# The down projection of a gated feed-forward network as seven half-size block products

## The reference, cut to what matters

```
f = silu(gc) * u
y = f @ w_down
x = layer_norm(ALPHA * x1 + gate2 * y) * ln2_g + ln2_b
```

## Time and profile before

| what | us |
|---|---|
| median of 3 runs | 2961.08 (2960.83 to 2962.52) |
| the profiled execution | 2957.33 |
| its span, first to last instruction | 2955.5 |
| TensorE busy in the span | 2721.9 |
| VectorE busy | 1767.3 |
| ScalarE busy | 1231.5 |
| GpSimd busy | 471.4 |

### The profile page before, as it was taken

The page is one execution under the profiler, slowest core; times in us unless marked ns, Lnnn a source line. Parts: engine busy times, 40 slices in busy tenths (PEclk is TensorE's granted clock), DMA queues, the critical chain, the costliest instruction groups (busy, mean ns, idle before and its releaser), DMA issues. The chain is left out here.

```text
span 2955.5 us, 50052 instructions
## 1 busy us (share of the span) xinstructions
PE 2721.9 (92%) x17011; PEld 2471.3 (84%) x17011; DVE 1767.3 (60%) x3030; ACT 1231.5 (42%) x2612; POOL 471.4 (16%) x678
## 2 busy tenths in 40 slices
PE   5999999766999987996999999999999979999996
PEld 4999999655887866885999999999999968888875
DVE  4534332155999984777887876667666534352445
ACT  2211111125988971233555565556555522112121
...
GB/s 289 83 93 120 79 92 64 165 359 178 128 151 124 163 47 147 189 190 98 213 174 172 171 206 153 151 154 151 152 151 151 109 173 141 107 128 138 84 122 135
DMA packets 400710, 435.71 MB, mean 147 GB/s; under 512 B 122593, under 2 KB 293655, under 8 KB 397849
## 3 DMA queue, kind: packets, MB, share of 16 engines
...
q0 software_dynamic: 2304, 7.88, 0.8%
...
## 5 line engine op out<-in xcount | busy, mean ns | idle before, releaser
L2204 PE MATMUL fu_alpha<-fu_h,fu_w 128*128 128x384 f32 x3168 | 574.0, 335 | 17.6 <-DVE fu_h L2430 10.6
L2690 PE MATMUL fd_acc<-fd_w,fd_f 128*128 128x512 f32 x2376 | 544.0, 390 | 29.7 <-DVE fd_w L2718 18.8
L2204 PEld LDWEIGHTS fu_alpha<-fu_h,fu_w 128*128 128x128 f32 x3168 | 552.8, 188 | 20.3 <-issue 20.2
L2690 PEld LDWEIGHTS fd_acc<-fd_w,fd_f 128*128 128x128 f32 x2376 | 446.0, 188 | 127.6 <-issue 18.3
L2204 PE MATMUL fu_beta<-fu_h,fu_w 128*128 128x384 f32 x1584 | 287.3, 336 | 0.6 <-DVE fu_h L2430 0.6
L2204 PEld LDWEIGHTS fu_beta<-fu_h,fu_w 128*128 128x128 f32 x1584 | 277.1, 189 | 1.1 <-issue 1.1
L598 PE MATMUL pj_gps<-pj_ht,w_in 128*128 128x256 f32 x2160 | 268.8, 285 | 0.0
L598 PEld LDWEIGHTS pj_gps<-pj_ht,w_in 128*128 128x128 f32 x2160 | 263.5, 191 | 1.3
L2714 DVE TENSOR_TENSOR fd_f<-fd_f_stage,fd_f 128x512 fp32r<-128x512 f32 (+1 forms) x110 | 88.9, 810 | 283.6 <-ACT fd_f L2670 283.6
L2670 ACT CAST fd_f<-fd_f_stage 128x512 fp32r<-128x512 f32 (+1 forms) x110 | 63.4, 579 | 442.8 <-PE fd_acc L2690 391.8
L2404 DVE TENSOR_TENSOR fu_w<-up_w_stage,fu_w 128x512 fp32r<-128x512 f32 x264 | 181.4, 688 | 86.0 <-ACT fu_w L2268 84.0
(11 more groups left out here) (221 smaller groups left out, 4123.3 us busy)
## 6 DMA issues: line engine op xcount, KB each, us to landing
...
at_k<-k_t SPq DMA_DIRECT2D x28, 704.0 KB, 12.9
...
```

Source lines behind the costliest of these rows:

```text
L2204: mm = pe.matmul(out, w[x][:, j, k, :], b[y][:, j, k, :], start=opens and (k, x, y) == (0, HI, HI), stop=(k, x, y) == (KH - 1, LO, HI), sk ...
L2690: mm = pe.matmul(acc[:, t, at], f[a][:, slot, t * P:(t + 1) * P], w[b][:, w_at(st, slot), at], start=is_step(st, 0) and (a, b) == (HI, HI) ...
```

## The change: what it does

The product is cut into blocks: `f` of each pair of token tiles into 2 x 2 (two tiles of 128 tokens, two halves of the 2816 rows), `w_down` into 2 x 2 (two halves of rows, two halves of 512 columns). In place of eight block products, Strassen's scheme makes seven, out of sums and differences of blocks (`A_OF` for `f`, `B_OF` for the weights), and each output block is a signed sum of some of the seven (`COPIES`, `SUMS`). The loops are turned about: one product at a time (order 2, 3, 1, 4, 5, 7, 6) runs through all nine pairs of tiles, so a unit is one product for one pair, 63 in all, with 11 k-steps of three passes. The outputs of all 18 tiles are summed up in SBUF (`fd_res`). For each unit SP loads one block of `f`, and a second one into the single buffer `fd_f_more` where VectorE has to sum two. Weight slices go round in a ring of 17; GpSimd sums two weight slices where needed. An output block is complete after products 4, 5, 7 and 6 (`complete`: gate, residual, statistics); after 7 and 6 a whole tile is, and is normalised by ScalarE (with a scale and a shift from GpSimd), multiplied and shifted by GpSimd (`affine`) and stored. The first unit and the first product's weights are loaded in three pieces of k-steps (`PIECES`), the weights from ScalarE's queue; the very last tile is normalised by VectorE (`last_tile`, two operations of 1024 columns). `slices` and `slices_first` say in which unit the next product's weight slices are made.

```diff
@@ -2539,245 +2539,406 @@
 def ffn_down_phase(nc, f_t, w_down, x1, ln2_g, ln2_b, mod, out_all):
...
-    KEPT = 14
...
+    PAIRS = T_ALL // (2 * P)
+    KH = FT // 2
+    NH = D // 2
+    ORDER = (2, 3, 1, 4, 5, 7, 6)
+    A_OF = {1: ((0, 0), (1, 1), ALU.add), 2: ((1, 0), (1, 1), ALU.add), 3: ((0, 0), None, None), 4: ((1, 1), None, None),
+            5: ((0, 0), (0, 1), ALU.add), 6: ((1, 0), (0, 0), ALU.subtract), 7: ((0, 1), (1, 1), ALU.subtract)}
+    B_OF = {1: ((0, 0), (1, 1), ALU.add), 2: ((0, 0), None, None), 3: ((0, 1), (1, 1), ALU.subtract),
+            4: ((1, 0), (0, 0), ALU.subtract), 5: ((1, 1), None, None), 6: ((0, 0), (0, 1), ALU.add), 7: ((1, 0), (1, 1), ALU.add)}
+    COPIES = {2: ((1, 0, 1.0), (1, 1, -1.0)), 3: ((0, 1, 1.0),), 1: ((0, 0, 1.0),)}
+    SUMS = {3: ((1, 1, ALU.add),), 1: ((1, 1, ALU.add),), 4: ((0, 0, ALU.add), (1, 0, ALU.add)),
+            5: ((0, 0, ALU.subtract), (0, 1, ALU.add)), 7: ((0, 0, ALU.add),), 6: ((1, 1, ALU.add),)}
+    COMPLETE = {4: (1, 0), 5: (0, 1), 7: (0, 0), 6: (1, 1)}
+    UNITS = len(ORDER) * PAIRS
+    PIECES = ((0, 2), (2, 6), (6, KH))
+    AHEAD = 6
+    RING = KH + AHEAD
+    WSLOTS, XSLOTS, HSLOTS, BANKS = 3, 3, 2, 8
+    STAGED_AT = 12
+    FIRST_COMPLETE = ORDER.index(4) * PAIRS
+    FIRST_TAIL = ORDER.index(7) * PAIRS
...
+        with nc.sbuf_tensor("fd_f_raw", [P, XSLOTS, KH, P], F32) as f_raw:
+            pass
+        f_lo = sb("fd_f_lo", [P, XSLOTS, KH, P], F32R)
+        f_hi = sb("fd_f_hi", [P, HSLOTS, KH, P], F32R)
+        f_more = sb("fd_f_more", [P, KH, P])
+        w = [sb(f"fd_w{h}", [P, RING, NH], F32R) for h in (HI, LO)]
+        wst = sb("fd_w_stage", [P, WSLOTS, 2, NH])
+        res = sb("fd_res", [P, 2 * PAIRS, D])
+        xr = sb("fd_x1", [P, 2, NH])
...
+        acc = ps("fd_acc", [P, BANKS, NH])
...
+        def slices_first(u):
+            j, i = divmod(u, PAIRS)
+            return [j * KH + k for k in (KH - 2, KH - 1)] if i == 0 and 0 < j < len(ORDER) else []
+        def slices(u):
+            j, i = divmod(u, PAIRS)
+            if j >= len(ORDER) - 1:
+                return []
+            if i == PAIRS - 1:
+                return [(j + 1) * KH + k for k in range(AHEAD, KH - 2)]
+            return [(j + 1) * KH + i - 2] if 2 <= i < 2 + AHEAD else []
...
+                def load_unit(u):
+                    if u >= XSLOTS:
+                        sp.wait_ge(unit_done, u - XSLOTS + 1)
+                    load_f(u)
+                    if sums_f(u) and u:
+                        sp.wait_ge(f_summed, sum_count(u) - 1)
+                        load_more(u, more_staged)
+                def load_w(b):
+                    s = (b - KH) % WSLOTS
+                    if b - KH >= WSLOTS:
+                        sp.wait_ge(w_low, b - WSLOTS + 1)
+                    first, second, _ = B_OF[ORDER[b // KH]]
+                    for at, block_of in enumerate((first, second)):
+                        if block_of is not None:
+                            kh, nh = block_of
+                            sp.dma_start(wst[:, s, at, :], w_blocks[kh, b % KH][:, half(nh)]).then_inc(w_staged[s], 16)
...
+                def store(u):
+                    sp.wait_ge(out_done, tail_count(u) + 1)
+                    sp.dma_start(out_tiles[tile_of(u)], res[:, tile_of(u), :]).then_inc(stored, 16)
+                load_unit(0)
+                load_unit(1)
...
+                for u in range(UNITS):
+                    if u + 2 < UNITS:
+                        load_unit(u + 2)
+                    for b in slices_first(u + 1) + slices(u + 1):
+                        load_w(b)
+                    if u >= FIRST_COMPLETE:
+                        load_x(u)
+                    if u - 3 >= FIRST_TAIL:
+                        store(u - 3)
...
+                def high_f(u, piece=0):
+                    k0, k1 = pieces(u)[piece]
+                    if sums_f(u):
+                        act.wait_ge(f_summed, sum_count(u, piece))
+                    else:
+                        act.wait_ge(f_staged[u % XSLOTS], 16 * f_loads(u))
+                    if u >= HSLOTS:
+                        act.wait_ge(unit_done, u - HSLOTS + 1)
+                    act.copy(f_hi[:, u % HSLOTS, k0:k1, :], f_raw[:, u % XSLOTS, k0:k1, :]).then_inc(f_high, 1)
...
+                    elif sums_w(b):
+                        act.wait_ge(w_summed, w_sum_count(b))
+                    else:
+                        act.wait_ge(w_staged[(b - KH) % WSLOTS], 16 * w_loads(b))
+                    if w_slot_free(b) is not None:
+                        act.wait_ge(slice_done, w_slot_free(b))
+                    act.copy(w[HI][:, b % RING, :], w_source(b)).then_inc(w_high, 1)
...
+                def normalise(u):
+                    n, t = tail_count(u), tile_of(u)
+                    act.wait_ge(shift_done, n + 1)
+                    act.activation(res[:, t, :], res[:, t, :], ACT.Identity, bias=shift[:, n % 4:n % 4 + 1],
+                                   scale=rstd[:, n % 4:n % 4 + 1]).then_inc(normed, 1)
...
+                for u in range(UNITS):
+                    for b in slices_first(u):
+                        high_w(b)
+                    if u + 1 < UNITS:
+                        high_f(u + 1)
+                    if u:
+                        first_terms(u - 1)
+                    for b in slices(u):
+                        high_w(b)
+                    if u - 2 >= FIRST_TAIL:
+                        normalise(u - 2)
+                normalise(UNITS - 2)
...
+                    for k in range(KH):
+                        begins = [n for n, (k0, _) in enumerate(pieces(u)) if k0 == k]
+                        if begins:
+                            pe.wait_ge(f_low, f_count(u, begins[0]))
+                        if i == 0:
+                            pe.wait_ge(w_low, j * KH + k + 1)
+                        at = (j * KH + k) % RING
+                        for a, b in PASSES:
+                            stationary = f_hi[:, u % HSLOTS, k, :] if a == HI else f_lo[:, u % XSLOTS, k, :]
+                            mm = pe.matmul(acc[:, u % BANKS, :], stationary, w[b][:, at, :], start=(k, a, b) == (0, HI, HI),
+                                           stop=(k, a, b) == (KH - 1, LO, HI))
+                        if i == PAIRS - 1 and k < KH - AHEAD:
+                            mm.then_inc(slice_done, 1)
+                    mm.then_inc(unit_done, 1)
...
+                def sum_f(u, piece=0):
...
+                        dve.wait_ge(f_staged[s], 16 * f_loads(u))
+                        dve.wait_ge(more_staged, 16 * (sum_count(u) - len(PIECES)))
+                    dve.tensor_tensor(f_raw[:, s, k0:k1, :], f_raw[:, s, k0:k1, :], f_more[:, k0:k1, :], A_OF[form(u)][2]).then_inc(f_summed, 1)
...
+                def low_f(u, piece=0):
+                    k0, k1 = pieces(u)[piece]
+                    dve.wait_ge(f_high, f_count(u, piece))
+                    dve.tensor_tensor(f_lo[:, u % XSLOTS, k0:k1, :], f_raw[:, u % XSLOTS, k0:k1, :],
+                                      f_hi[:, u % HSLOTS, k0:k1, :].bitcast(F32), ALU.subtract).then_inc(f_low, 1)
+                def low_w(b):
+                    dve.wait_ge(w_high, b + 1)
+                    dve.tensor_tensor(w[LO][:, b % RING, :], w_source(b), w[HI][:, b % RING, :].bitcast(F32), ALU.subtract).then_inc(w_low, 1)
+                def later_terms(u):
+                    dve.wait_ge(unit_done, u + 1)
+                    for r, nh, op in SUMS.get(form(u), ()):
+                        if COPIES.get(form(u)) or u < 4 * PAIRS:
+                            dve.wait_ge(copied, copy_count(u))
+                        at = res[:, 2 * pair(u) + r, half(nh)]
+                        dve.tensor_tensor(at, at, acc[:, u % BANKS, :], op).then_inc(added, 1)
+                    if form(u) in COMPLETE:
+                        complete(u)
+                def complete(u):
+                    r, nh = COMPLETE[form(u)]
+                    t, n = tile_of(u), complete_count(u)
+                    at = res[:, t, half(nh)]
                     dve.wait_ge(consts_loaded, 64)
...
+                    dve.wait_ge(added, add_count(u))
+                    dve.tensor_tensor(at, at, gate[:, vec(t), half(nh)], ALU.mult).then_inc(gated, 1)
+                    dve.wait_ge(gated, n + 1)
+                    dve.wait_ge(x_staged[n % 2], 16 * (n // 2 + 1))
+                    dve.scalar_tensor_tensor(at, xr[:, n % 2, :], ALPHA, at, ALU.mult, ALU.add).then_inc(res_done, 1)
+                    dve.wait_ge(res_done, n + 1)
+                    dve.bn_stats(stats[:, t, nh * 6:nh * 6 + 6], at).then_inc(stats_done, 1)
+                    if u >= FIRST_TAIL:
                         dve.wait_ge(stats_done, n + 1)
...
+                        dve.tensor_copy(waited[:, :], stats[:, t, 0:1])
+                        m = tail_count(u)
+                        dve.bn_aggr(mv[:, m % 4, :], stats[:, t, :]).then_inc(mv_done, 1)
...
```

(59 more changed lines are left out.)

293 lines of the change are left out of this document (116 added, 177 removed).

## The result

The kernel after takes 2974.87 us (median of 5 runs, 2967.08 to 2976.37), the kernel before 2961.55 in the same series: ratio 1.0036, 95% interval 1.0024 to 1.0047. Forecast were 2947 us and 14 us less. The profiled execution of after took 2967.08 us, its span is 2965.3, against 2955.5 before: 9.8 us more. It is the shortest of the five.

A forecast was written before the change was run, and what follows sets the result against it. Phase bound by TensorE's matmul count; start to 2410, 453 us of units, 12 lost in product 5, 49 in products 7 and 6, 17 tail: span 2941 against 2955.5, so median 2947 us, range 2915 to 2985.

The forecast's parts named there:

- Matmuls: TensorE in this phase: 2079 matmuls in place of 2376, at 225.2 ns each, 63 units of 7.43 us, 468.2 us.
- Start: First units: 5.0 MB at 293 to 386 GB/s must land first; unit 2 begins near 2410, bounds 2400 and 2416.
- The first three seams: Changes of product 2-3, 3-1, 1-4: VectorE stands for late weight slices, 2 to 5 us of slack take this; no cost.
- Product 5: Its units and both seams: VectorE's 7.6 us a unit exceeds TensorE's 7.43; 12 us lost, bounds 3 and 17.
- the collision with a weight sum: Product 5: a VectorE op waits for one GpSimd weight sum, 0.8 us added per unit in six units.
- Products 7 and 6: Last 15 units: VectorE and GpSimd exclude each other, units of 11.2 and 9.65 us; 49 us lost, bounds 0 and 83.
- the lock: VectorE and GpSimd ops on two SBUF tiles never overlap; in product 7, 10.9 us of holds against a 7.43 us unit.
- Tail: After the last matmul: output work, last normalising and store, 17 us against 16.1 before; bounds 13 and 20.
- Loads: Rival, chance 0.18: VectorE's sum of f waits for its second load in products 2 or 1; 27 us more, 2974.
- Clock: Rival, chance 0.04: TensorE's gaps in products 7 and 6 drop its clock to 1.2 GHz; 64 us more, 3011.

The follow-up runs named there:

- e3_start: Changed kernel with first weight pieces queued on SP behind their f pieces and constants loaded in product 3; 2969.07 us, ratio to before 1.0022.
- e8_ring: Changed kernel with GpSimd writing weight sums straight into the ring of low parts, freeing staging slots earlier; 2958.66 us, ratio to before 0.9988.
- e2: Changed kernel with GpSimd's two passes per tile (scale, shift) replaced by five fills that only write SBUF; 2952.59 us in one run.
- e1_no_affine: Changed kernel without GpSimd's two passes per tile (times ln_g, plus ln_b); 2938.72 us in one run.
- e4_seam: Changed kernel with five first-block and two second-block weight staging slots, slices 9 and 10 loaded before the next f load; 2970.61 us, ratio to before 1.0032.
- e10_fill: Changed kernel with eight extra matmuls, results overwritten, ahead of each product's second unit and unit 2; 2965.02 us, ratio to before 1.0012.

## Why the prediction went wrong

The forecast span was 2941, the measured one 2965.3. The medians, 2947 and 2974.87, lie 3.6 us further apart: that part is in the runs without a trace. Term by term:

- **Matmuls** (468.2): right in number; the pace was 0.7% off. 222 in 50 us counts the two that the window's edges cut; 63 units at 7.48 are 3 us more. The same error stood in the reading of before (22 us lost, in truth 18.7).
- **Start** (unit 2 at 2410): 2416. Counted against the first matmul, 19.3 lost for 13, 6.3 us more, 1.8 of them unit 2's half clock. The sum took bytes over a rate; the sums of f wait for the last block in a queue. e3_start gives 3 to 5 us of it back.
- **The first three seams**, "At the first three seams 2 to 5 us of slack take this": the step that failed. They cost 11.7 us, about half of the whole error. The late load was seen and put on VectorE, and at the later seams it was priced (3, 6.1 and 15.6 us; measured 4.1, 10.1 and 13.8). At the first three it was set against VectorE's free time in a unit. But TensorE does not wait for VectorE's work of a unit to be done; it needs slice 9 inside the same unit and low f, which stands behind the low parts in VectorE's queue, at its end. At 3-1 these were waits of 2.14 and 1.73 us, and most of the rest of its 6.7 is the low clock behind them. e8_ring, which loads the two slices 5 us earlier, takes the three seams to 3.3, so the cause is shown.
- **Product 5** (12): 15.0 with both seams. The size was near by luck: "here VectorE becomes the bound by itself" fails. The inner units run at 7.48 to 7.84 and lose 0.8, not 6; VectorE is busy for 34.0 of 38.6 us there (2705.2 to 2743.8), and gate and residual take 0.69, so the collision with a weight sum did not come. The seams cost 14.1, not 9.1.
- **Products 7 and 6** (49): 47.4 up to the last matmul. Place and size were right, and near in each part: product 7 costs 19.1 (units 48 to 53), the seam 13.8 (54 and 55), product 6 14.6; forecast were 21.8, 15.6 and 11.8, with one unit more at product 7's pace and one less at product 6's. Gate and residual wait in product 7, as it was stepped through; the sign named for it, means of low f and sum of f well over 1.62, holds for low f in product 6 alone. e2 shows the lock by itself in product 6. In product 7 GpSimd's chain is long enough to cost something without it (9.4 us with fills, e2), so there the lock's share is not shown alone. Of the 47.4, e1_no_affine takes away 28; 14 stay at the seam, 5 in other units.
- **Tail** (17): 17.2.

That is 3 + 6.3 + 11.7 + 3 - 1.6, and 1.4 for the later first matmul and 0.2 in the tail: 24, the whole difference. With start and first seams at their measured size the sum is 2959, on the other side of 2955.5; with the seams alone it is 2953, still below.

**Loads**, the slower rival, gave 2974, nearly what was measured, but by accident: its sign came, its cost did not. In products 2, 1 and 5 VectorE's sum did wait for the second block, up to 3.3 us, and beside it the units ran at 7.48 in products 2 and 1, at 7.48 to 7.84 in product 5. A sum's wait cost time at the start, in e4_seam behind a blocked queue, and in e1_no_affine, where the lock was eased. **Clock** was priced at units wholly at the low level and set aside. It came at the gaps, some 1.6 us each in a dozen units, in the last stretch too (unit 57), where it hid behind the lock as forecast. Where no wait of VectorE hides it, it counts: about 10 us by the medians of e10_fill. TensorE waited in products 3 and 4 as well, at their seams, where the prediction saw no reason.

The four unprofiled runs of after are 7 to 9 us above the profiled one. The first matmul of the phase came between 2382.7 and 2387.6 in the nine traces that leave the start as it is, and the clock steps differ; whether that is all of it stays open. So does what remains of the seam 7-6 (11 to 12.5 us in the best two).
